# One sum buffer per modulation chunk in the opening, convolution taps issued singly, and the convolution's layer norm spread over the attention passes

## The reference

```python
c_act = silu(c)
mod = c_act @ mod_w[i] + mod_b[i]                 # 9 x 1024 columns per layer
h = modulate(rmsnorm(x, norm_g[i, 0]), sh1, sc1)  # needs the first 2048 of them
...
def conv_module(u, dw_w, dw_b, ln_g, ln_b, pw_w):
    a, gt = split(u, 2)
    v = a * sigmoid(gt)
    v = depthwise_conv(v, dw_w, width=31) + dw_b
    mu = mean(v, axis=-1); xc = v - mu            # over the 1024 channels
    v = silu(xc * rsqrt(mean(xc * xc, axis=-1) + EPS) * ln_g + ln_b)
    return v @ pw_w
...
y = sigmoid(g_conv) * conv_out + sigmoid(g_attn) * nsa_out
return y @ w_out
```

## Time and profile before

| what | us |
|---|---|
| median of 3 runs | 1995.94 (1994.97 to 1999.92) |
| the profiled execution | 2001.47 |
| its span, first to last instruction | 1998.8 |
| PE busy | 1771.5 (89% of the span) |
| DVE busy | 1292.2 (65%) |
| ACT busy | 873.7 (44%) |
| POOL busy | 43.4 (2%) |

### The profile page before, as it was taken

The page is one execution under the profiler, slowest core; times in us unless marked ns, Lnnn a source line. Parts: engine busy times, 40 slices in busy tenths (PEclk is TensorE's granted clock), DMA queues, the critical chain, the costliest instruction groups (busy, mean ns, idle before and its releaser), DMA issues.

```text
span 1998.8 us, 31881 instructions
## 1 busy us (share of the span) xinstructions
PE 1771.5 (89%) x11498; PEld 1590.5 (80%) x11498; DVE 1292.2 (65%) x2171; ACT 873.7 (44%) x1400; POOL 43.4 (2%) x77
## 2 busy tenths in 40 slices
PE   3699988758999979997798999978999889889997
PEld 3599968646899969996587999878977578769996
DVE  2777776656778777776455555568689665455553
ACT  1344444413444444444465544445355544544442
POOL 1000000000000000000000000010000000000000
PEclk9999989968899989998899999989899989889998
DMA  7588844804788858874332466535333145425661
GB/s 298 197 277 291 293 140 129 219 0 162 254 286 289 281 190 283 288 248 127 98 124 64 158 188 184 164 124 162 114 103 91 43 145 172 127 64 182 186 188 64
DMA packets 107956, 349.52 MB, mean 175 GB/s; under 512 B 9514, under 2 KB 36154, under 8 KB 98528
## 3 DMA queue, kind: packets, MB, share of 16 engines
q1 hardware_dynamic: 93488, 262.18, 41.3%
q10 hardware_dynamic: 12432, 78.65, 11.6%
q0 software_dynamic: 1952, 7.57, 1.2%
HBM read 344.16 MB, written 4.19 MB: 174 GB/s over the span
## 4 chain that ended last, share of the span: by engine, by line
PE 79%; DVE 9%; ACT 5%; issue 3%; DMA 2%; POOL 1%; ACTq 0%; DVEq 0%; SPq 0%; POOLq 0%
PE ps L622 66%; DVE w_lo L184 2%; DVE arena L304 2%; PE ps L500 2%; PE ps L312 1%; ACT w_hi L178 1%; PE ps L2135 1%; PE ps L2215 1%; DMA arena<-in_small 1%; DMA raw<-in_stream 1%; PE ps L1476 1%; ACT arena L369 1%; PE ps L1537 1%; DVE arena L1139 1%; PE ps L342 1%
## 5 line engine op out<-in xcount | busy, mean ns | idle before, releaser
L622 PE MATMUL ps<-t_hi,w_hi 128*128 128x256 f32 x2488 | 721.8, 290 | 16.5 <-DVE t_lo L2320 6.1
L622 PE MATMUL ps<-t_lo,w_hi 128*128 128x256 f32 x2488 | 714.1, 287 | 0.0
L622 PE MATMUL ps<-t_hi,w_lo 128*128 128x256 f32 x2488 | 713.3, 287 | 0.0
L622 PEld LDWEIGHTS ps<-t_hi,w_hi 128*128 128x128 f32 x2488 | 485.3, 195 | 31.8 <-issue 19.5
L622 PEld LDWEIGHTS ps<-t_lo,w_hi 128*128 128x128 f32 x2488 | 485.2, 195 | 3.7 <-issue 1.0
L622 PEld LDWEIGHTS ps<-t_hi,w_lo 128*128 128x128 f32 x2488 | 484.8, 195 | 0.7
L184 DVE TENSOR_TENSOR w_lo<-raw,w_hi 128x1024 fp32r<-128x1024 f32 x240 | 290.7, 1223 | 221.5 <-ACT w_hi L178 221.2
L880 DVE TENSOR_TENSOR w_lo<-raw,w_hi 128x1024 fp32r<-128x1024 f32 x258 | 313.8, 1224 | 158.6 <-ACT w_hi L869 158.6
L869 ACT ACTIVATE w_hi<-raw 128x1024 fp32r<-128x1024 f32 x258 | 269.3, 1053 | 176.3 <-PE ps L622 176.3
L178 ACT ACTIVATE w_hi<-raw 128x1024 fp32r<-128x1024 f32 x240 | 249.2, 1054 | 181.3 <-PE ps L622 172.5
L304 DVE SCALAR_TENSOR_TENSOR arena<-arena,cact 128x512 f32<-128x512 f32 x252 | 188.8, 749 | 5.8
(11 more groups left out here) (285 smaller groups left out, 1706.2 us busy)
## 6 DMA issues: line engine op xcount, KB each, us to landing
raw<-in_stream SPq DMA_DIRECT2D x498, 512.0 KB, 4.3
arena<-in_mod_w ACTq DMA_DIRECT2D x72, 1024.0 KB, 7.0
u_scratch<-u_keep ACTq DMA_DIRECT2D x1, 3072.0 KB, 34.5
arena<-u_scratch POOLq DMA_DIRECT2D x8, 256.0 KB, 3.2
small<-in_small POOLq DMA_DIRECT2D x1, 1368.0 KB, 24.9
resid<-in_x POOLq DMA_DIRECT2D x1, 1024.0 KB, 17.1
arena<-in_mem POOLq DMA_DIRECT2D x1, 1024.0 KB, 5.2
out<-resid SPq DMA_DIRECT2D x1, 1024.0 KB, 4.0
```

Source lines behind the costliest of these rows:

```text
L622: last = TE.matmul(out, lhs, rhs, start=start and i == 0, stop=stop and i == 2)
```

## The change

1. *Opening.* Each of the four chunks has a sum buffer of its own (`modp_first`: `modp`, the two halves of `tmp`, one of `act_s`) and its own four columns of PSUM bank 7, so that no chunk waits for the sum of the one before. DVE's queue holds the products of chunks 0 and 1, the normalisation's scaling, two splits, the products of chunks 2 and 3, and one addition for all four. PE's queue holds turn 0, the 62 matmuls of the bias tables, turns 1 to 3. The copies of the tables come after the first norm (`bias_keep`).
2. *Taps.* Work is handed out one tap at a time. A call after a split or a compression product issues three taps, a call in a step of the passes two, and only before step 16; 124 taps in all, as before.
3. *Layer norm.* `channel_sums` takes the filler's place on PE in steps 16 and 21, in a bank of the filler (which runs to step 29 so). Mean and centring stand in steps 16 to 19, the squares with them. The inverse deviation is computed by POOL as a power over 128 x 256, issued at step 21; DVE's rescales stand in steps 24 to 27. Silu and split follow the passes, and the gates' sigmoids come behind them in eight pieces.

The diff, cut:

```diff
+        modp_first = [modp, tmp[:, 0, :], tmp[:, 1, :], act_s[:, 0, :]]
...
+                total = modp_first[c] if first else modp
...
+            total, at = (modp_first[c], 4 * c) if first else (modp, 0)
             for j in range(4):
-                last = TE.matmul(ps[7][:, j:j + 1], modp[:, j * P:(j + 1) * P], cs("ones", 0, 1), start=True, stop=True)
+                last = TE.matmul(ps[7][:, at + j:at + j + 1], total[:, j * P:(j + 1) * P], cs("ones", 0, 1), start=True, stop=True)
...
+        def bias_keep(at):
...
             @block.vector
             def _(dve):
-                dve.wait_ge(T.sem, T.n)
-                dve.wait_ge(used, blocks["pe"])
+                dve.wait_ge(T.sem, at)
                 VE.tensor_copy(u_keep[:, :], ps[0][0:16, 0:384]).then_inc(V.sem, V.up())
...
+        normalize(lambda q: x[:, q, :], lambda q: ar(XN, QT, D)[:, q, :], first_norm, landed_first=inputs, scale_after=2)
+        for _i in range(2):
+            next_split()
+        @block.vector
+        def _(dve):
+            for c in range(2, PRE):
+                mod_products(dve, c, range(KT), first=True)
+        @block.tensor
+        def _(pe):
+            pe.wait_ge(first_in.sem, first_in.n)
+            mod_turn(pe, 0, first=True)
+        bias_at = bias_products()
+        @block.tensor
+        def _(pe):
+            for c in range(1, PRE):
+                mod_turn(pe, c, first=True)
+        @block.vector
+        def _(dve):
+            dve.wait_ge(mod_cols, PRE)
+            VE.tensor_tensor(modc[:, 0:4 * PRE], ps[7][:, 0:4 * PRE], col("mod_b", 0, 4 * PRE), ALU.add).then_inc(mod_added, PRE)
...
         norm_x(lambda k, n: col("norm_g", k, n), (mod_at(0, 0), mod_at(0, 1)), ready=first_norm, mods_before=PRE)
+        bias_keep(bias_at)
+        turned["at"] = (V.n, A.n)
...
-        pending = [(pair, lo, min(31, lo + TAPS)) for pair in range(KT // 2) for lo in range(0, 31, TAPS)]
+        pending = [(pair, k, k + 1) for pair in range(KT // 2) for k in range(31)]
...
+        def three_taps():
+            for _i in range(3):
+                next_taps()
+        meanwhile.append(three_taps)
...
+        def deviation_step():
+            @block.vector
+            def _(dve):
+                dve.wait_ge(T.sem, sums_done[0])
+                VE.tensor_scalar(rstd, sum_bank(1)[:, 0:L], 1.0 / D, EPS, ALU.mult, ALU.add).then_inc(V.sem, V.up())
+            sum_read[SUM_AT[1] // 4 + 1] = V.n
+            at = V.n
+            @block.gpsimd
+            def _(pool):
+                pool.wait_ge(V.sem, at)
+                GE.tensor_tensor(rstd, rstd, st[:, 60:61].to_broadcast([P, L]), ALU.pow).then_inc(G.sem, G.up())
+        def rescale(pr):
+            @block.vector
+            def _(dve):
+                dve.wait_ge(G.sem, G.n)
+                VE.tensor_tensor(by_pair(cv, pr), by_pair(cv, pr), rstd.unsqueeze(1).to_broadcast([P, 2, L]),
+                                   ALU.mult).then_inc(V.sem, V.up())
...
+        chores = {16: [mean_step], 17: [lambda: centre(1)], 18: [lambda: centre(2)], 19: [lambda: centre(3)],
+                  21: [deviation_step], 24: [lambda: rescale(0)], 25: [lambda: rescale(1)], 26: [lambda: rescale(2)],
+                  27: [lambda: rescale(3)]}
...
-            fill_half()
+            if step == SUM_AT[0]:
+                assert not pending
+                channel_sums(cv, sum_bank(0), (V.n, fill_free[SUM_AT[0] // 4 - 1]))
+            elif step == SUM_AT[1]:
+                channel_sums(square, sum_bank(1), (0, max(squares_at[0], fill_free[SUM_AT[1] // 4 - 1])))
+            else:
+                fill_half()
...
-            next_taps()
+            for work in chores.get(step, ()):
+                work()
+            if step < SUM_AT[0]:
+                next_taps()
+                next_taps()
...
-        @block.scalar
-        def _(act):
-            act.wait_ge(V.sem, V.n)
-            E.activation(rstd, rstd, ACT.Sqrt).then_inc(A.sem, A.up())
-        @block.vector
-        def _(dve):
-            dve.wait_ge(A.sem, A.n)
-            VE.reciprocal(rstd, rstd).then_inc(V.sem, V.up())
...
+        for pr in range(4):
+            conv_split(pr)
+        for v in (gattn, gconv):
             for pr in range(4):
+                @block.scalar
+                def _(act):
+                    E.activation(by_pair(v, pr), by_pair(v, pr), ACT.Sigmoid).then_inc(A.sem, A.up())
```

More of the change, by code:

```diff
@@ L382, in _ @@
             def _(dve):
+                if scale_after:
+                    dve.wait_ge(first_in.sem, first_in.n)
+                    dve.wait_ge(A.sem, silu_at)
+                    for c in range(scale_after):
+                        mod_products(dve, c, range(KT), first=True)
                 for q in range(QT):
@@ L1914, in build @@
             silu_at[kind] = A.n
-            next_taps()
+            three_taps()
         @block.gpsimd
@@ L1982, in _ @@
                         pe.wait_ge(A.sem, fill_free[pair - 2])
+                    if half == 0 and pair in sum_read:
+                        pe.wait_ge(V.sem, sum_read[pair])
                 for k in range(4 * part, 4 * part + 4):
@@ L2227, in pass_keep, with channel_sums @@
             o_kept[pr] = A.n
-        for step in range(N_PASS + 2):
-            n = step - 1
-            if 0 <= n < N_PASS:
-                pass_scale(n)
-            if step < N_PASS:
-                pass_scores(step)
-            fill_half()
-            fill_lo()
-            if 0 <= n < N_PASS:
-                pass_turn(n)
-            if step >= 2:
-                pass_values(step - 2)
-                if (step - 2) % 4 == 3:
-                    pass_keep((step - 2) // 4)
-            fill_keep()
-            next_taps()
-        fill_lo()
-        assert fill_at[0] == 32 and not fill_todo and not lo_todo
-        while pending:
-            next_taps()
-        def channel_sums(src, bank):
+        square = cin[:, :, 0:L]
+        mean, rstd = biasc_free[:, 0, :], biasc_free[:, 1, :]
+        sums_done = {}
+        def channel_sums(src, bank, ready):
             @block.tensor
             def _(pe):
-                pe.wait_ge(V.sem, V.n)
-                pe.wait_ge(A.sem, A.n)
+                pe.wait_ge(V.sem, ready[0])
+                pe.wait_ge(A.sem, ready[1])
                 for k in range(KT):
@@ L2303, in build, with conv_split @@
         conv_hi = {}
-        for pr in range(4):
+        def conv_split(pr):
             two = slice(2 * pr, 2 * pr + 2)
@@ L2321, in build, with _ @@
             kt_ready[2 * pr] = kt_ready[2 * pr + 1] = (V.n, conv_hi[pr])
+        for step in range(N_PASS + 2):
+            n = step - 1
+            if 0 <= n < N_PASS:
+                pass_scale(n)
+            if step < N_PASS:
+                pass_scores(step)
+            if step == SUM_AT[0]:
[5 more added lines that the diff above has]
+                fill_half()
+            fill_lo()
+            if 0 <= n < N_PASS:
+                pass_turn(n)
+            if step >= 2:
+                pass_values(step - 2)
+                if (step - 2) % 4 == 3:
+                    pass_keep((step - 2) // 4)
+            fill_keep()
+            for work in chores.get(step, ()):
[3 more added lines that the diff above has]
+                next_taps()
+        fill_lo()
+        assert fill_at[0] == 32 and not fill_todo and not lo_todo
+        for pr in range(4):
+            conv_split(pr)
+        for v in (gattn, gconv):
+            for pr in range(4):
+                @block.scalar
+                def _(act):
+                    E.activation(by_pair(v, pr), by_pair(v, pr), ACT.Sigmoid).then_inc(A.sem, A.up())
+                if v is gattn:
+                    @block.vector
+                    def _(dve):
+                        dve.wait_ge(A.sem, A.n)
+                        VE.tensor_tensor(by_pair(gattn, pr), by_pair(gattn, pr), by_pair(qT, pr), ALU.mult).then_inc(V.sem, V.up())
+                else:
+                    conv_gate[pr] = A.n
         y_hi = {}
```

108 lines of the change are left out of this document (43 added, 65 removed).

## The result

The changed kernel takes 2006.01 us (median of 10 runs), the kernel before 1995.12 (10 runs): ratio 1.0043, 95% interval 1.0026 to 1.0059. In later rounds of the same two programs it was 1.0061 (1.0040 to 1.0082). The forecast was 1999 us. The profiled execution took 2005.77 us, its span is 2003.7. One execution in this document, of the kernel with the power over 128 columns, took 2910.85 us at a granted clock of 0.557; its median and its ratio leave it out.

The account below looks back on a forecast made before the run. PE was taken as the bound (79% of the span), so only its waits could give time back. Terms -21.3 + 6.4 + 6.6 - 16.8 = -25.1, plus 28.4 for POOL's power, gave +3.3 us: 1999 us, range 1968 to 2010.

Parts of the forecast that it names:

- Opening, -21.3: At the kernel's start: PE's bias products wait only for mod turn 0, so the transposes start earlier; net -21.3 us.
- The bounds of -18 and -23: Opening's limits: -18 us if raw blocks sharing DMA with mod chunk 4 come late, -23 if table copies fall into a gap.
- Taps, +6.4: Before the passes: DVE's 7.36 us per tile pair against PE's 5.76 makes PE wait, mostly in the first projection; +6.4 us.
- End, -16.8: Last value matmuls to second projection: 4.4 us remain of 21.2, since the layer norm moves into the passes; -16.8 us.
- Passes without POOL, +6.6: Attention passes: two sums replacing half fills, a wait for DVE's queue and two fills put off cost +6.6 us.
- Power, +28.4: Steps 21 to 25: POOL's power takes 39.8 us, PE idles 27, plus 1.4 for lower clock behind it; +28.4 us.
- a short power (1971 us): Layer norm on POOL: a power of up to 12.9 us stays hidden under steps 22 to 24; 1971 us, chance 0.25.
- A slope that falls with length: POOL's power: cost per column falls, 13 to 31 us in all, stall only beyond 12.9; 1971 to 1990 us, chance 0.17.
- the power at 256 ns a column: POOL's power slower, PE idles 52.7 us around step 24; 2025 us, chance 0.10.
- Rival 4: Power as forecast, but the taps cost +11 us and the opening gives only 18; 2007 us, chance 0.08.

Follow-up runs that it names:

- the two single edits: The kernel before with only the changed opening: 1974.26 us, ratio 0.9887; the kernel before with only the taps' new handing out: 2000.91 us, ratio 1.0025.
- the early silu: First pair's silu and split on ACT put ahead of the attention result's last copy, against the kernel with root and reciprocal: 1971.45 us, ratio 0.9884.

## Why the prediction was right, and where its terms were off

The forecast of no change to slightly slower (1999 us, range 1968 to 2010) holds, and so does its mechanism: five terms, each found where it was said to be. The range was wide and reached from a clear gain to a loss, so that the time falls into it says little; and the chances had faster (0.47) ahead of slower (0.28). Term by term:

- **Opening, -21.3:** measured -21.1 by itself. The bounds of -18 and -23 weren't needed. DVE waited 0.8 us for one mod chunk and PE ended its bias products at 40.48 instead of 39.95, which cancelled against an earlier turn of the first chunks.
- **Taps, +6.4:** measured +5.5. The waits of PE were forecast as 0.6, 1.6, 1.6, 1.6 and came as 0.6, 1.3, 1.35, 1.2, the 1.0 near the softmax as 0.9. DVE's period was 7.36 us to the hundredth. The long ones are shorter than forecast because PE takes 6.02 us for a pair behind a wait (from 1348.08), not 5.76.
- **End, -16.8:** right by itself. The second projection starts 4.36 us behind the last values, where 4.4 were said.
- **Passes without POOL, +6.6:** too small by 2 to 3 us. From the first scores to the end of the last values it is 118.6 us in the kernel before and 127.7 to 127.8 in the four profiles without a stall: +9.2. The sums cost 5.0 (forecast 5.1) and the two fills put off about 1 (forecast 1.5). The rest is PE at the lower clock, which the forecast put at nothing: the 27 matmuls of one early step take 7.17 us at a granted clock of 0.52 in the changed kernel, 4.23 at 1.00 in the kernel before, and in two of the profiles the last values take 2.7 instead of 1.5. The handing out of the taps alone adds 0.5 of it, which stands in the +5.5 already.
- **Power, +28.4:** this is the term that was mis-sized most. The duration was good: 41.2 for 39.8 us, and PE's wait 28.6 for 27. The step "I add 1.4 for the lower clock behind it" failed: the steps behind the wait lost 3.4 to 4.2 us. 1.4 is about what a stretch of 3 us at half the clock loses, as in the earlier trace rows; here PE ran nearly 10 us at a granted clock of 0.53. Measured in place 31.0 to 33.4, between ratios 33.8.

By the traces and the two single edits this is -21.1 + 5.5 + 8.7 - 16.8 = -23.7 without the stall, where the ratios say 0.98825, so -23.4. With 31.0 to 33.4 for the stall the sum is +7.3 to +9.7 us; the direct comparison says +8.6 (0.43% of 1995) in one set of rounds and +12.2 in the other. The forecast's +3.3 is 5 to 9 us short of that, most of it in the stall and some in the passes.

The rivals: a short power (1971 us) was wrong as a fact and right as a price, since the kernel with 64 columns, where it is hidden, takes 1972.1. A slope that falls with length didn't occur, nor did the power at 256 ns a column. Rival 4 has 2007 us, nearer to the measured 2006 than the forecast, but its terms (taps +11, opening -18) came as +5.5 and -21.1: that the numbers meet is chance. 64, 128 and 256 columns take 10.568, 20.764 and 41.165 us, 159 ns for each column more, at both steps. That four columns took 1.02 us was the sign of it: 460 ns for three columns are 153. The Trainium skill (GPSIMD Engine Reference, 3.1 Elementwise) gives about 2.6 cycles per element for a two-input elementwise operation. The trace does not agree for a power: by that page, as an estimate, 256 columns would be near 1 us, and they took 41.2.

In the page's 40 slices the one that holds the end of the passes has 8 tenths for PE, not 5 as it says ahead of the prediction; 5 is the digit of PEld, the weight loads. The argument rests on the timeline and not on it.

The Trainium skill (TensorE: Matmul & The Clock Gate, Part 1) says that the array falls to 1.2 GHz when idle. The trace agrees, with a granted clock of 0.50 while PE stands and 0.53 in the 10 us after.

## What to carry to other kernels

Moving work to an idle engine is only free if nobody on a busy engine waits for it in order: one instruction of DVE that waited for POOL held 30 us of softmax, because the queue behind it is the kernel's chain. Put the reader of a slow result as late as the order allows (here steps 24 to 33, worth 33 us between medians), and check that the result is there by then: here the power just filled the steps left. Or compute it the short way. And price a stall of PE with the slow steps behind it, not with its length alone: here 3.4 to 4.2 us, for a wait of 8 us as for one of 28.

Between two stages in which the same engine has no room to spare, moving work brought nothing, however visible the waits were that vanished: here 5.4 us of waits went and 7.9 came in the passes. The variants with late rescales, or with root and reciprocal and the early silu, are 1.2 to 1.4% below the kernel before (ratios 0.9864 to 0.9885) and 1.7% below the changed one.

## What the runs showed of the hardware that was not expected

- A power on POOL costs 159 ns a column of 128 values, linear from 64 to 256 columns; a root on ACT and a reciprocal on DVE over the same tile take 0.42 and 1.75 us, plus two table loads of 1.28.
- POOL busy with that power did not slow the passes: five steps took 18.83 us beside it and 18.83 without.
- Behind a wait of 8.2 us PE lost 4.0 us by the lower clock, behind 28.55 us it lost 4.1 and 3.4.
- The same instructions, from the first projection to the second sums, took 237.9 to 238.0 us in three executions and 242.4 to 242.7 in five. In the two profiles of one kernel the whole difference is PE's busy time at another granted clock (0.95 and 0.93). A profile of one execution can mislead by that much.
